# Half of attention's output projection moved between the levels of the delta rule's inverse

## The reference, cut to what matters

```python
p_att, p_rwkv, p_gate = split(rms_norm(x, pre_mix_g) @ w_in)          # p_gate + gate_bias
y_a = chunk_band_attention(q, k, v, rel_bias)                          # 512 wide
y_b = rwkv7_time_mix(p_rwkv, ...)                                      # 512 wide, delta rule, then a norm by head
gate_a, gate_b = sigmoid(p_gate[..., :1024]), sigmoid(p_gate[..., 1024:])
merged = gate_a * (y_a @ proj_a) + gate_b * (y_b @ proj_b)
x = x + rms_norm(merged @ w_out, post_mix_g)
```

## Time and profile before

| | us |
|---|---|
| median of 3 runs | 2098.3 |
| lowest, highest | 2097.86, 2099.78 |
| span of the profiled execution | 2095.3 |
| PE busy in the span | 2069.4 |
| stage `rwkv_chunks`, from its first transposes to its last state | about 274 to 390 |
| stage `merge`: gates and norm, then projections | 390 to 423, 423 to 466 |

### The profile page before, as it was taken

How to read it: one execution, slowest core, us unless ns; L and a number is a source line. 1 busy time by engine, 2 the same in 40 slices (tenths; PEclk the granted TensorE clock), 3 DMA queues, 4 the chain that set the end, 5 groups by cost and what they waited for, 6 DMA issues and landing times.

```text
span 2095.3 us, 31362 instructions
## 1 busy us (share of the span) xinstructions
PE 2069.4 (99%) x12912; PEld 1681.1 (80%) x12912; DVE 897.6 (43%) x1497; ACT 890.2 (42%) x1678; POOL 896.3 (43%) x690
## 2 busy tenths in 40 slices
PE   9999999999999999999999999999999999999998
PEld 7777778888888888877777888888877788888886
DVE  5331765453510121353337644442257774444222
ACT  4444743453532342254345544442245544444322
POOL 5523320154444445544232544445454264444443
PEclk9999999999999999999999999999999999999999
DMA  7222210142233233222121222233222123222321
GB/s 274 101 79 93 71 38 14 37 151 91 81 100 101 90 101 101 71 91 71 51 71 42 80 96 94 93 101 101 101 71 91 41 81 101 91 92 100 103 99 61
DMA packets 53591, 184.13 MB, mean 88 GB/s; under 512 B 5816, under 2 KB 5824, under 8 KB 53320
## 3 DMA queue, kind: packets, MB, share of 16 engines
q1 hardware_dynamic: 53448, 182.13, 26.1%
HBM read 176.84 MB, written 8.15 MB: 88 GB/s over the span
## 4 chain that ended last, share of the span: by engine, by line
PE 94%; DVE 3%; ACT 1%; issue 1%; POOL 1%; DMA 0%; SPq 0%; POOLq 0%; DVEq 0%; ACTq 0%
PE ps L361 22%; PE ps L363 22%; PE ps L362 22%; PE ps L2826 2%; PE ps L2828 2%; PE ps L2827 2%; PE ps L387 2%; PE ps L381 1%; PE ps L382 1%; PE ps L1167 1%; PE ps L507 1%; PE ps L1169 1%; PE ps L1168 1%; PE ps L479 1%; PE ps L1693 1%
## 5 line engine op out<-in xcount | busy, mean ns | idle before, releaser
L201 POOL TENSOR_TENSOR split_units<-raw_units,split_units 128x512 fp32r<-128x512 f32 x628 | 822.2, 1335 | 1077.5 <-ACT split_units L178 1061.7
L178 ACT ACTIVATE split_units<-raw_units 128x512 fp32r<-128x512 f32 x624 | 356.8, 621 | 353.1 <-PE ps L363 315.3
L361 PE MATMUL ps<-x_split,split_units 128*128 128x512 f32 x1208 | 474.9, 393 | 1.7 <-DVE work L2476 0.8
L363 PE MATMUL ps<-x_split,split_units 128*128 128x512 f32 x1208 | 470.2, 389 | 0.0
L362 PE MATMUL ps<-x_split,split_units 128*128 128x512 f32 x1208 | 470.1, 389 | 0.0
L361 PEld LDWEIGHTS ps<-x_split,split_units 128*128 128x128 f32 x1208 | 226.8, 188 | 54.1 <-issue 4.0
L362 PEld LDWEIGHTS ps<-x_split,split_units 128*128 128x128 f32 x1208 | 226.8, 188 | 47.6 <-issue 1.4
L363 PEld LDWEIGHTS ps<-x_split,split_units 128*128 128x128 f32 x1208 | 226.8, 188 | 47.1
L361 PE MATMUL ps<-hidden_split,split_units 128*128 128x512 f32 x608 | 237.3, 390 | 0.0
L363 PE MATMUL ps<-hidden_split,split_units 128*128 128x512 f32 x608 | 236.6, 389 | 0.0
L362 PE MATMUL ps<-hidden_split,split_units 128*128 128x512 f32 x608 | 236.5, 389 | 0.0
(11 more groups left out here) (538 smaller groups left out, 3264.9 us busy)
## 6 DMA issues: line engine op xcount, KB each, us to landing
raw_units<-stream SPq DMA_DIRECT2D x314, 512.0 KB, 3.3
work<-gate_rows SPq DMA_DIRECT2D x12, 256.0 KB, 2.9
bias_rows<-bias_line SPq DMA_DIRECT2D x1, 2816.0 KB
gate_rows<-work SPq DMA_DIRECT2D x10, 256.0 KB, 2.1
x<-x_t SPq DMA_DIRECT2D x4, 512.0 KB, 6.5
work<-bias_rows SPq DMA_DIRECT2D x1, 2048.0 KB
out_t<-x SPq DMA_DIRECT2D x8, 256.0 KB
vec<-vectors SPq DMA_DIRECT2D x1, 1159.5 KB, 6.0
```

Source lines behind the costliest of these rows:

```text
L178: scalar.activation(self.split[:, u % SPLIT, 0, part], self.raw[:, u % RING, part], ACT.Copy).then_inc(self.high_done, 1)
L201: gpsimd.tensor_tensor(self.split[:, u % SPLIT, 1, part], self.raw[:, u % RING, part], self.split[:, u % SPLIT, 0, part].bitcast(F32), ALU ...
L361: TE.matmul(out, high, rhs(0, k), start=(k == 0), stop=False)
L363: ins = TE.matmul(out, low, rhs(0, k), start=False, stop=last and shift is None)
```

## The change

In each chunk, twelve more dense matmuls make attention's projection for one even output tile (`EARLY_FIRSTS = (0, 2, 4, 6)`, one for each chunk): four right after `bonus`, then one after each `level_u` of levels 1 to 4, which is eight in all. ACT copies the product to a work tile, SP stores it in memory, and at the start of `merge` SP loads the four of them. `merge` then has 12 projection tiles in place of 16, and for even `m` DVE multiplies the loaded tile, not a bank. The split of `y_a` into high and low parts moves from ACT and DVE in `merge` to POOL at the start of `rwkv_chunks`. The weights are reordered: one unit is now half a gate tile and one projection tile, so two units more are rounded and subtracted in `rwkv_chunks` and two fewer in `merge`.

```diff
+                def first_half(ch):
+                    out = bank(GATE_BANK)
+                    pe.wait_ge(read_act.sem, read_act.at(2 * ch + 1))
+                    for k in range(KH):
+                        last = k == KH - 1
+                        if ch == 0:
+                            pe.wait_ge(norm_low2.sem, norm_low2.at(k + 1))
+                        high, low = wts.take(pe)
+                        TE.matmul(out, high, attended(0, k), start=(k == 0), stop=False)
+                        yield
+                        TE.matmul(out, high, attended(1, k), start=False, stop=False)
+                        yield
+                        ins = TE.matmul(out, low, attended(0, k), start=False, stop=last)
...
                     bonus(ch)
+                    dense = first_half(ch)
+                    for _ in range(AFTER_BONUS):
+                        next(dense)
                     for l in range(1, TOP):
                         level_t_x(l, 0, l, ch)
                         level_u(l, 0, ch)
+                        next(dense)
                         if l < TOP - 1:
                             level_t_x(l, 1, l + 1, ch)
                             level_u(l, 1, ch)
+                            next(dense)
                     level_t_x(TOP - 1, 1, TOP, ch)
                     level_u(TOP - 1, 1, ch)
+                    next(dense)
                     level_x(TOP, 1, ch)
...
-                    pe.wait_ge(read_act.sem, read_act.at(ch + 1))
+                    pe.wait_ge(read_act.sem, read_act.at(2 * ch + 2))
                     solve(0, 0, ch)
...
+                def stage_first(ch):
+                    if ch >= 2:
+                        act.wait_ge(first_spilled[ch % 2], 16)
+                    act.wait_ge(tile_ready.sem, tile_ready.at(2 * ch + 2))
+                    S.activation(w[:, FIRST_AT[ch % 2], :], bank(GATE_BANK), ACT.Copy).then_inc(read_act.sem, 1)
...
-                        if ch < 2 and l < 3:
+                        if l < 3:
                             wts.round_half(act, S)
+                    stage_first(ch)
...
+                highs = [pool_chain.mark(G.tensor_copy(attended(0, t), w[:, YA + t, :])) for t in range(KH)]
+                for t in range(KH):
+                    pool.wait_ge(pool_chain.sem, highs[t])
+                    G.tensor_tensor(attended(1, t), w[:, YA + t, :], attended(0, t).bitcast(F32), ALU.subtract
+                                    ).then_inc(norm_low2.sem, 1)
...
+                    wait_dve(sp, 1, ch, dve_level(TOP, "u"))
+                    wts.load(sp, u0 + ch + SPLIT + RING)
+                    sp.wait_ge(read_act.sem, read_act.at(2 * ch + 2))
+                    sp.dma_start(gate_rows[FIRSTS_ROW + ch], w[:, FIRST_AT[ch % 2], :]
+                                 ).then_inc(first_spilled[ch % 2], 16)
...
+                for n in range(len(EARLY_FIRSTS)):
+                    sp.wait_ge(first_spilled[n % 2], 16 * (n // 2 + 1))
+                    sp.dma_start(w[:, FIRSTS[n], :], gate_rows[len(GATE_ROWS) + n]).then_inc(first_landed, 16)
...
-                for t in range(4):
-                    high_in(YA + t)
...
-                for t in range(4):
-                    low_in(YA + t, t + 1)
...
+                    if m in EARLY_FIRSTS:
+                        first = w[:, FIRSTS[EARLY_FIRSTS.index(m)], :]
+                    else:
+                        dve.wait_ge(tile_ready.sem, tile_ready.at(number["projection", m, 0]))
+                        first = bank_of("projection", m, 0)
                     dve.wait_ge(read_act.sem, read_act.at(2 * m + 1))
-                    V.tensor_tensor(mg, bank_of("projection", m, 0), ga, ALU.mult).then_inc(dve_out.sem, 1)
+                    V.tensor_tensor(mg, first, ga, ALU.mult).then_inc(dve_out.sem, 1)
```

More of the change, by code:

```diff
@@ L296, in network @@
         gate_landed = [sem(f"gate_landed_{i}") for i in range(4)]
+        first_spilled = [sem(f"first_spilled_{i}") for i in range(2)]
+        first_landed = sem("first_landed")
         con_landed, vec_landed, bias_landed = sem("con_landed"), sem("vec_landed"), sem("bias_landed")
@@ L1533, in network, with attended @@
         LAST = LEVELS - 1
+        def attended(half, k):
+            return attended_low[:, k, :] if half else attended_high[k // 2][:, k % 2, :]
         def stage_rwkv_chunks():
@@ L2064, in _ @@
                 ins.then_inc(zero_out2.sem, 1)
[L2065 to L2067 removed]
+                highs = [pool_chain.mark(G.tensor_copy(attended(0, t), w[:, YA + t, :])) for t in range(KH)]
[3 more added lines that the diff above has]
+                                    ).then_inc(norm_low2.sem, 1)
+                for ch in range(NT):
+                    wts.subtract_low(pool, G, u0 + ch + SPLIT)
+                    if ch % 2:
+                        sum_halves(ch // 2)
             @block.sync
             def _(sp):
[L2071 to L2078, removed]
+                for ch in range(NT):
+                    if ch % 2:
+                        j = ch // 2
+                        sp.wait_ge(norm_pool.sem, norm_pool.at(j + 1))
+                        sp.dma_start(gate_rows[FIRST_ROW + j], staged[:, j, :]
+                                     ).then_inc(row_done(FIRST_ROW + j)[0], 16)
+                    wait_dve(sp, 1, ch, dve_level(TOP, "u"))
[3 more added lines that the diff above has]
+                                 ).then_inc(first_spilled[ch % 2], 16)
+            tile_ready.close(2 * NT)
+            read_act.close(2 * NT)
+            norm_low2.close(KH)
             norm_pool.close(2)
@@ L2099, in stage_merge @@
             order = [(kind, m, j) for kind, m in merge_order() for j in range(2)
-                     if kind != "gate" or (m, j) not in GATE_ROWS]
+                     if ((m, j) not in GATE_ROWS if kind == "gate" else j or m not in EARLY_FIRSTS)]
             number = {p: n + 1 for n, p in enumerate(order)}
@@ L2103, in stage_merge @@
             for kind, m, j in order:
-                unit_of[kind, m, j] = n
-                n += 1 if kind == "gate" or j == 1 else 0
+                unit_of[kind, m, j] = n // UNIT
+                n += KD if kind == "gate" else KH
             def bank_of(kind, m, j):
                 return bank((0 if kind == "gate" else 4) + 2 * (m % 2) + j)
-            def part(a):
-                return lambda half, k: mix_split[:, half, a + k, :]
+            parts = (attended, of(mix_split))
             def norm_mean(pe):
@@ L2155, in _ @@
                         pe.wait_ge(dve_out.sem, dve_out.at(2 * (m - 2) + j + 1))
-                    src = (KD, of(xs)) if kind == "gate" else (KH, part((4, 0)[j]))
+                    src = (KD, of(xs)) if kind == "gate" else (KH, parts[j])
                     split_product(pe, bank_of(kind, m, j), *src, tile_ready, n + 1, among[n] if n in among else None)
@@ L2166, in _ @@
             def _(sp):
+                for out in (act_out, act_out2):
+                    sp.wait_ge(out.sem, out.at(0))
+                for n in range(len(EARLY_FIRSTS)):
+                    sp.wait_ge(first_spilled[n % 2], 16 * (n // 2 + 1))
+                    sp.dma_start(w[:, FIRSTS[n], :], gate_rows[len(GATE_ROWS) + n]).then_inc(first_landed, 16)
                 for m, j in by_tile:
                     n = GATE_ROWS.index((m, j))
-                    wts.load(sp, u0 + unit_of["projection", m - 2, 0] + 1 + RING)
+                    wts.load(sp, u0 + unit_of["projection", m - 2, 1] + 1 + RING)
                     sp.wait_ge(dve_out.sem, dve_out.at(2 * (m - 2) + 2))
```

40 lines of the change are left out of this document (25 added, 15 removed).

## The result

| | before | after |
|---|---|---|
| median of five runs, us | 2097.94 | 2104.01 |
| lowest, highest | 2097.70, 2099.78 | 2099.88, 2107.34 |
| span of the profiled execution | 2095.3 | 2100.3 |

The change makes the kernel slower: ratio 1.0029, 95% interval 1.0018 to 1.0039, that is +6.1 us. The profiled execution took 2102.06, one of the better ones, with 5.0 us more span than the one of before. These 5.0 us are found first, by cutting the trace at the same four places as the earlier trace rows.

The account below looks back on a forecast made before the run. PE, busy for 99% of the span, was taken to bound the kernel. Chunks +11.8, merge -10.9 and a wait of +1.4 gave +2.3 us on 2098.3, so 2100.6 us, likeliest "same"; range 2093.0 to 2105.5.

Parts of the forecast that it names:

- (b): Chunks: PE drains in full at each change of tile size, 0.72 per single dense matmul; 2105.1 us, chance 0.10.
- (c): Merge: gate rows bind instead of PE, each pair of tiles costing 10.9 us, PE waiting 6.5; 2105.7 us, chance 0.10.
- Removed from the merge: Merge projections: 48 dense matmuls at 0.227 us leave PE's path, saving 10.9 us.
- After `bonus`: Each chunk, after `bonus`: PE has no gap there, so four dense matmuls at 0.23 cost their full 0.92 us.
- Between the levels: Chunk levels: a single dense matmul takes 0.58 in a 0.34 gap; seven places lose 0.24, the eighth 0.35, 2.03 us.
- (a): Chunk levels: dense matmuls vanish in PE's gaps, only the four after `bonus` cost; 2092.5 us, chance 0.17.
- A chunk: Each chunk grows by 0.92 after `bonus` plus 2.03 between levels, 2.95 us; 11.8 us for four.
- (d): Chunk 0: dense matmuls wait for POOL's split of `y_a`, PE waiting 3.7 in all; 2104.3 us, chance 0.06.
- The last merged tile: Merge end: the gate rows' return makes tile pairs take 9.2 us, so PE waits 1.4 us at `w_out`.
- SP stores four tiles: nothing waits behind them: Chunks: SP's four new tile stores delay only later stores and loads of units, costing 0.
- A wait costs its length: Chunks and merge: granted clock read as 1.00, PE's waits priced by length alone, as 1.4 us at `w_out`.
- (slower): Whole kernel: outcome slower than the "same" band of 2094.1 to 2102.5, by (b), (c) or (d); chance 0.26.

Follow-up runs that it names:

- eight slots and late store: The change with eight merge gate slots instead of four, and each chunk's tile store moved into the next chunk's levels: 2097.54 us, ratio 1.0003.
- eight slots: The change with eight gate slots in the merge instead of four, the store staying at its chunk's end: 2098.78 us, ratio 1.0008.
- no stores: The change with its four tile stores left out, the merge loading four gate rows in their place: 2102.30 us, ratio 1.0021.
- forced wait: The kernel before, with DVE making the last merged tile's low part four more times before reporting it: 2102.92 us, ratio 1.0029.
- late load: The change with eight gate slots and the next unit's 512 KB load, not the store, moved into the next chunk's levels: 2097.48 us, ratio 1.0003.

## Why the prediction was right or wrong

The time lies in the range; the case named as likeliest, no change, does not hold. That the range held is in part luck: its upper end was set for (b) and (c), neither of which happened. Step by step:

- **Removed from the merge**, 10.9: 10.88. Right.
- **After `bonus`**, 0.92 a chunk: from `bonus` to PE's next product 280.61 to 282.59, 1.98, before 1.05; 0.93. Right.
- **Between the levels**, 0.24 a place from a single dense matmul of 0.58: right, put together from the row of four.

```profile
283.11 0.63 PE L1725 MATMUL ps<-work 64*64 64x64 f32 x16
283.67 0.50 PE L1669 MATMUL ps<-attended_low,split_units 128*128 128x512 f32 x1
284.10 0.27 PE L1721 MATMUL ps<-work 64*64 64x64 f32 x2
```

The last small start is 283.11 + 0.63 - 0.22 = 283.52; to 284.10 are 0.58. This refutes (a), 0.34, and (b), 0.72. The half-level period of 1.52 against 1.27 says 0.25. The Trainium skill (TensorEngine Tiling (Array Packing), Tiling Modes) says that a change of tiling mode drains the TensorE; here such a change cost what rows 5 gave, not what the records' ends would give.
- **A chunk**, 2.95: 3.07 in chunk 0 of the version with eight slots and late store (32.18 - 29.11), which has neither break nor fall. Not foreseen: the small breaks of the kernel before, 1.13 us by their records, are gone where gaps are filled. So that version's four chunks, from the first `bonus` to the merge, cost 120.43 - 109.20 = 11.2, not 11.8.
- **ACT, the weights' units, the new wait of `solve`**, 0: PE's waits for ACT in the chunks add up to 1.6 us, before to 1.4. **POOL's split**, 0: right. Its copies took 2.35 for four, and the last low part was there at 281.23; (d) did not happen.

```profile
273.91 2.35 POOL L2106 CAST attended_high<-work 128x512 fp32r<-128x512 f32 x4
276.23 5.00 POOL L2109 TENSOR_TENSOR attended_low<-work,attended_high 128x512 fp32r<-128x512 f32 x4
```

- **The last merged tile**, 1.4: the step is right in kind and too small. A pair was to take 9.2; it took 9.4 on average, so PE waited 1.97 us in the first profile (1.81 of them idle), and was idle for 1.6 to 2.7 in the others. The gate rows' return is the cause, as forecast: with eight slots the wait is gone. (c) asked for 10.9 a pair throughout. The Trainium skill (GPSIMD Engine Reference, Specifications) says that POOL contends with a DVE instruction of two SBUF inputs; the even product's 1.67 beside POOL agrees, against 0.69 without. How much of the wait is this, and how much ACT's late copy, no run separates.
- **"SP stores four tiles: nothing waits behind them"**, 0: this step failed. I looked for who waits on the stores' queue, and not at who else uses the DMA engines then. By the counts above, PE's own instructions do. It cost 1.0 to 1.1 us in chunk 0, and 1.6 to 1.7 more where the clock fell. So chunk 0 grew by twice as much as the others, the sign that was set for (d), without (d).
- **A wait costs its length**: the second step that failed. I took the granted clock of 1.00 as given, while a standstill of PE can cost 1.6 to 1.7 us more behind it. The sum without both is the prediction's: 11.2 - 10.9 + 2.0 = +2.3. With the break of 1.0 it is +3.3, and the profile of the change run again, which has no fall, is 3.4 longer than that of before. The longer runs, up to 2107, probably have more falls: their mean clocks are lower (0.995 to 0.997, where the lowest runs have 0.999). Where these lie no profile shows.

So (slower) came true by none of the four rivals, but by two prices left out of the forecast's own case.

## What to carry to other kernels

A new wait of a fully busy TensorE is to be priced twice: by its length, and by what it costs if the clock falls behind it, here 1.6 to 1.7 us more; in these profiles it fell behind some waits and not behind others. Work that is moved into an engine's gaps still pays for the change of shape, so compare one start-to-start row with the gap before counting on it. And a store that nobody waits for is not free when it lengthens a burst in front of an instruction fetch: split the burst, or move one transfer into a quiet stretch.

## What the runs showed of the hardware that was not expected

- PE's instructions arrive in blocks of 16 KB, one for about 127 matmuls: every 4 us or so among 64x64 matmuls, up to 31 us apart in dense stages. The profile counts them among the transfers of the core's 16 DMA engines. In chunk 0, 768 KB of data in front of a block stopped PE for 0.76 to 0.93 us, and 512 KB did not; 768 KB that met the blocks otherwise (chunks 1 to 3) did not either.
- Long runs of 64x64 matmuls have breaks of 0.2 to 0.5 us without any semaphore, each ending 1.2 to 1.5 us after a block of instructions has landed; no version with a dense matmul after each half level has them.
- The granted clock fell to 0.50 behind standstills of PE of 0.9 us (the change, chunk 0), 2.7 us (no stores) and 3.3 us (forced wait), and did not behind others of 0.8, 0.9, 1.7 and 1.8 us, nor behind the one of 1.75 us that all twelve profiles have at the start of the chunks. It also fell in two profiles with no standstill ahead (eight slots and late load, at about 1624), at a cost of 1.5 us.
- A DVE product of two operands in SBUF took 0.69 us alone and 1.67 beside POOL; one with an operand in PE's banks took 0.69 beside POOL too.
